# Order of the last expert pages and passes of both MoE layers: down page 30 asked for first, expert 31's gate/up page in halves of k

## What is computed

```python
def expert_block(args):
    xb, e = args
    hb = jax.nn.silu(xb @ w_gate[e]) * (xb @ w_up[e])
    return hb @ w_down[e]
...
    h = h + hierarchical_moe(rmsnorm(h, norm_ffn[layer]), ...)
return rmsnorm(h, final_norm)
```

## Time and profile before

| | |
|---|---|
| median of 3 runs | 1268.96 us (1267.98 to 1270.03) |
| the profiled execution's own time | 1268.41 us |
| its span, first to last instruction | 1266.7 us |
| mean granted TensorE clock | 0.902 of full speed |
| PE busy | 1040.9 us (82%) |
| HBM read | 459.38 MB, 364 GB/s over the span |
| the expert stream of layer 0, its end | about 531 to 569 us |
| the expert stream of layer 1, its end | about 1221 to 1259 us |

### The profile page before, as it was taken

How to read it: one execution, slowest core, us unless ns; L and a number is a source line. 1 busy time by engine, 2 the same in 40 slices (tenths; PEclk the granted TensorE clock), 3 DMA queues, 4 the chain that set the end, 5 groups by cost and what they waited for, 6 DMA issues and landing times.

```text
span 1266.7 us, 22370 instructions
## 1 busy us (share of the span) xinstructions
PE 1040.9 (82%) x9525; PEld 704.6 (56%) x9525; DVE 478.3 (38%) x1230; ACT 234.8 (19%) x526; POOL 4.9 (0%) x27
## 2 busy tenths in 40 slices
PE   9999998866767575889999999999967675758676
PEld 7888755533433342448888888876533333425243
DVE  2342543532223222237665556464343222222223
ACT  2221121111111111103433333121111111111111
POOL 1000000000000000000000000000000000000000
PEclk9999998978788877899999999999988878878789
DMA  9888799999999999996676664899999999999997
GB/s 342 237 338 332 255 419 429 426 428 428 429 429 428 429 429 427 417 394 187 190 231 225 229 223 151 334 361 427 428 427 427 430 428 429 427 429 429 429 419 297
DMA packets 98305, 461.49 MB, mean 364 GB/s; under 512 B 17468, under 2 KB 60728, under 8 KB 73400
## 3 DMA queue, kind: packets, MB, share of 16 engines
q1 hardware_dynamic: 97872, 460.34, 90.5%
q10 hardware_dynamic: 360, 0.15, 0.0%
HBM read 459.38 MB, written 1.08 MB: 364 GB/s over the span
## 4 chain that ended last, share of the span: by engine, by line
PE 51%; DMA 45%; SPq 1%; DVE 1%; issue 1%; ACT 1%; POOL 0%; POOLq 0%; DVEq 0%; ACTq 0%
DMA front<-in_expert_w_up 39%; PE pa L1534 10%; PE pa L1829 8%; PE pb L1534 8%; DMA arena<-in_expert_w_down 5%; PE wa L1829 5%; PE acc L1565 4%; PE wb L1859 3%; PE acc L1684 2%; PE pb L1609 1%; SPq L362 1%; PE pb L1903 1%; PE wa L2124 1%; PE pb L1785 1%; PE acc L1869 1%
## 5 line engine op out<-in xcount | busy, mean ns | idle before, releaser
L1829 PE MATMUL pa<-front,arena 128*32 128x256 f32 x1792 | 126.6, 445 | 80.8 <-DMA front<-in_expert_w_up 80.8
L1289 DVE TENSOR_SCALAR lower<-lower 128x128 f32<-128x128 f32 x64 | 14.4, 225 | 417.6 <-ACT lower L606 417.6
L1829 PE MATMUL wa<-front,arena 128*32 128x256 f32 x1232 | 96.7, 479 | 88.5 <-DMA front<-in_expert_w_up 85.0
L1829 PEld LDWEIGHTS pa<-front,arena 128*32 128x32 f32 x1792 | 63.0, 128 | 146.9 <-DMA front<-in_expert_w_up 93.6
L1829 PEld LDWEIGHTS wa<-front,arena 128*32 128x32 f32 x1232 | 46.1, 136 | 142.1 <-DMA front<-in_expert_w_up 95.0
L606 ACT ACTIVATE arena<-wb 32x256 f32<-32x256 f32 (+2 forms) x236 | 88.9, 377 | 105.0 <-PE wb L1859 96.6
L1859 PE MATMUL wb<-w_dn,conv_raw 128*32 128x256 f32 x1472 | 87.9, 379 | 2.3 <-DMA w_dn<-in_expert_w_down 2.0
L1534 PE MATMUL pa<-hnT,w_x 128*128 128x256 f32 x384 | 85.1, 380 | 0.0
L1829 PE MATMUL wa<-w_x,arena 128*32 128x256 f32 x896 | 64.4, 451 | 19.1 <-DMA w_x<-in_expert_w_up 19.1
L1534 PEld LDWEIGHTS pa<-hnT,w_x 128*128 128x128 f32 x384 | 72.5, 190 | 10.0 <-issue 0.3
L1534 PE MATMUL pb<-hnT,w_x 128*128 128x256 f32 x336 | 74.5, 380 | 0.0
(11 more groups left out here) (345 smaller groups left out, 1252.0 us busy)
## 6 DMA issues: line engine op xcount, KB each, us to landing
w_dn<-in_expert_w_down SPq DMA_DIRECT2D x46, 2048.0 KB, 26.4
front<-in_expert_w_gate SPq DMA_DIRECT2D x42, 2048.0 KB, 19.1
front<-in_expert_w_up SPq DMA_DIRECT2D x42, 2048.0 KB, 23.6
w_x<-in_expert_w_gate SPq DMA_DIRECT2D x15, 2048.0 KB, 32.2
w_x<-in_expert_w_up SPq DMA_DIRECT2D x15, 2048.0 KB, 36.6
arena<-in_expert_w_down SPq DMA_DIRECT2D x14, 2048.0 KB, 25.8
w_x<-in_odd_in_proj SPq DMA_DIRECT2D x16, 1024.0 KB, 5.5
front<-in_expert_w_up SPq DMA_DIRECT2D x10, 1024.0 KB, 8.8
```

Of the source, the lines that this page charges most:

```text
L1289: link(v.tensor_scalar(eg, eg, 1.0, None, ALU.add))
L1829: ins = mm(gu[32 * j:32 * j + 32, :, :], xb[:, k, c0:c0 + CAP], w[k][:, :, P * j:P * j + P], start=(k == 0), stop=(k == KC - 1))
```

## The change

- SP: down 30 is asked for right after up 29, ahead of the wait in `overflow_weights`. After it come gate/up 30, then gate/up 31 in four DMAs of 1024 KB (gate and up for k 0 to 3, then gate and up for k 4 to 7), then down 31 in its two parts.
- PE: gate/up 31 is two passes of half the k, each behind the wait for its half (`gu_res`, `gu_in1`). Down 30 runs ahead of gate/up 31, where the six matmuls on zeros stood, and sum 30 behind gate/up 31.
- ACT: the copy of down 30's result stands ahead of expert 31's exponential.
- SP: the wait for the last part of down 31 before the load of fnorm is gone.

```diff
                 last = [(e, expert_at(l, e)) for e in (NE - 2, NE - 1)]
+                expert_part(l, NE - 2, 2, NE * l + previous(DSLOT, NE - 2), last[0][1])
                 overflow_weights(l)
                 k1 = sp_.value_load(table[0:1, l + 1:l + 2], min_val=0, max_val=OV_LIST)
                 sp_.wait_ge(S["ov_done"], k1 + 1)
-                for parts in ((0, 1), (2,)):
-                    for e, which in last:
-                        for part in parts:
-                            expert_part(l, e, part, NE * l + previous(DSLOT if part == 2 else SLOT, e), which)
+                for part in range(2):
+                    expert_part(l, NE - 2, part, NE * l + previous(SLOT, NE - 2), last[0][1])
+                sp_.wait_ge(S["gu_done"], NE * l + previous(SLOT, NE - 1) + 1)
+                for half in range(2):
+                    k = slice(KC // 2 * half, KC // 2 * half + KC // 2)
+                    for part in range(2):
+                        w = (expert_w_gate, expert_w_up)[part][l, ds(last[1][1], 1), :, :]
+                        sp_.dma_start(w_gu[SLOT[NE - 1]][:, part, k, :],
+                                      w.rearrange("a (p k) f -> p (a k) f", k=KC)[:, k, :]
+                                      ).then_inc(S[("gu_res", "gu_in1")[half]], 16)
+                expert_part(l, NE - 1, 2, NE * l + previous(DSLOT, NE - 1), last[1][1])
...
             sp_.wait_ge(S["gu_done"], 2 * NE - 2)
-            sp_.wait_ge(S["dn_in3b"], 2 * uses(DSLOT, 3, NE) * 16)
             sp_.dma_start(fnorm, final_norm.partition_broadcast(P)).then_inc(S["fnorm_in"], 16)
...
-                    if e == NE - 1:
-                        output_alone(l, e - 1)
+                    if e == NE - 2:
+                        output_alone(l, e)
...
+                    if e == NE - 1:
+                        pe.wait_ge(S["gu_res"], 48 * l + 48)
+                        gate_up(xs, CAP * j, gu_cols(s), GU[e % 2], ks=range(KC // 2))
...
+                    elif e == NE - 1:
+                        gate_up(xs, CAP * j, gu_cols(s), GU[e % 2], ks=range(KC // 2, KC)).then_inc(S["gu_done"], 1)
...
-                    if e and e != NE - 2:
+                    if e and e < NE - 2:
                         down_of(l, e - 1)
...
                     if e == NE - 2:
-                        warm(6)
+                        down_of(l, e)
```

More of the change, by code:

```diff
@@ L1975, in moe @@
                     if e == 3:
-                        pe.wait_ge(S["gu_res"], 16 * l + 16)
+                        pe.wait_ge(S["gu_res"], 48 * l + 16)
                     if e == WIDE:
```

## The result

| | before | changed |
|---|---|---|
| median, same chip | 1269.44 us (12 runs, 1266.91 to 1271.6) | 1273.7 us (12 runs, 1270.12 to 1275.93) |
| ratio | | 1.0031, interval 1.0022 to 1.0041 |
| the profiled execution | 1268.41 us, span 1266.7 | 1273.96 us, span 1272.2 |

The change makes the kernel 2.8 to 5.2 us slower (0.0022 and 0.0041 of 1269.44): 3.9 us by the ratio, 4.3 by the two medians. The forecast was 1271.9, +2.9 us on its own baseline.

The account below looks back on a forecast made before the run. The expert pages' DMA stream was taken to set the pace, with PE waiting. Terms 0.1 + 0.9 - 0.1 + 2.0 = +2.9 us on 1268.96 gave 1271.9 us, range 1269.2 to 1274.4.

Parts of the forecast that it names:

- The stream: Expert pages at layer ends: same bytes and queue, new order, so the last landing stays; 0 us taken.
- the dip: DMA rate falling to 315 and 360 GB/s at SP's return, 0.8 us of missing bytes; filling it counted 0.
- the larger end (0.9 us): Other bound for filling the dip: last landing 0.9 us earlier in layer 0, 0.4 in layer 1.
- Rival 3: Early down 30 fills the dip, later landings come 0.9 and 0.4 us earlier; 1268.6 with clock up, chance 0.10.
- Gate/up 30 lands later: Its page comes third behind up 29; PE idles 2.9 us in layer 0, 1.5 us in layer 1.
- The chain behind it: From gate/up 30 through down 30 and gate/up 31 to down 31's end: +0.1 us layer 0, +0.9 layer 1.
- The clock in layer 0: The 2.9 us gap ahead of gate/up 30 mostly makes that pass slow, by 1.4 to 2.7 us; +2.0 taken.
- Rival 1: The clock stays up in layer 0; total +0.9, 1269.9 us, chance 0.27.
- The clock in layer 1: The 1.5 us gap ahead of gate/up 30 leaves the clock up; 0 taken, 2.7 us as other end.
- Rival 2: The clock falls in both layers; total 4.9, 1273.9 us, chance 0.15.
- The halves "save 1.8 us": Splitting gate/up 31 lets it start before down 30's old landing place; saves 1.8 us on the way.
- The final norm's load: Asked for right behind down 31, it has landed before DVE needs it at the end; -0.1 us, at most -0.2.

Follow-up runs that it names:

- warm_l0: The changed kernel with 12 matmuls on zeros ahead of gate/up 30 in layer 0 only; 1272.71 us, ratio 1.0024 to before.
- whole_page: The changed kernel with gate/up 31 in one piece, without the first half pass and its wait; 1273.80 us, ratio 1.0030 to before.
- down30_early_only: The kernel before with only down 30 asked for ahead of the wait on down pass 27; 1276.06 us, ratio 1.0052 to before.
- fnorm_early_only: The kernel before without the wait on down 31 ahead of the final norm's weight load; 1269.01 us, ratio 0.9995 to before.
- change_third: The changed kernel as it is, profiled a third time; one profile, 1269.59 us.
- halves_only: The kernel before with gate/up 31 as four 1024 KB DMAs and two half passes; 1270.65 us, ratio 1.0011 to before.

## Why the prediction was right, and where it was not

The forecast was slower, +2.9 us; measured +3.9, inside the range, with the mechanism that was named. That the three profiles come to 2.7 is in part luck. In layer 0 they have +0.2 of chain and +1.9 of clock, near the +0.1 and +2.0 of the sum. In layer 1 they have +0.2 of chain, where +0.9 was taken (against before's two ends, one of them 0.8 late), and +0.4 of clock, where 0 was: errors that partly cancel.

- **The stream: right.** The last landing did not move with the dip. The 0 for it holds; the larger end (0.9 us) does not. Over all fourteen profiles, in the seven ends with a dip (some 2 us under 360 GB/s between 8 and 2 us before up 29 lands) it came 29.48 to 30.13 us behind up 29, in 20 of the 21 without one 29.40 to 30.48, in the last 31.09. Rival 3 is out. The Trainium skill ("DMA: Bandwidth & Descriptors", "Rules for kernel authors") advises to issue a DMA early and to wait for it late; here down 30 did come early, and no reader needed it so.
- **Gate/up 30 lands later: right to 0.2 us.** It starts 14.66 to 14.92 us behind up 29, on its page. The gap in layer 0 was foreseen at 2.9 us; it was 2.65 to 4.40, as PE is early there when gate/up 29 runs fast.
- **The chain behind it: right in size.** From gate/up 30's start to the end of down 31 the prediction put 567.6 - 550.9 = 16.7 us for layer 0; in the changed layer 1 it is (1261.53 + 1.07) - 1246.04 = 16.6. The +0.1 of layer 0 was too small by the luck of the baseline: that layer's last landing was the latest of before's four (30.13). Against 29.71 + 2.77 it is 0.5. The +0.9 of layer 1 was too large: up 29 was put at 1226.6 by counting pages back from down 30, but landed at 1226.10, so gate/up 30 came 0.5 us sooner behind it than the sum has. With the clock up it is 32.94 - 32.58 = 0.4.
- **The clock in layer 0: right.** +2.0 was taken, from a slow pass of 1.4 to 2.7; measured 1.3 to 2.5 over 3.66, in three profiles of three. Rival 1 got 0.27 because one row in five had stayed fast; but the five are not alike. The one that stayed fast follows full-size sums, the one at 462.06 matmuls on 32 rows:

```profile
411.81 3.72 PE L1869 MATMUL acc<-arena 128*128 128x256 f32 x16 [0.61 <-ACT arena L606]
418.00 3.66 PE L1829 MATMUL pa<-front,arena 128*32 128x256 f32 x64 [2.48 <-DMA front<-in_expert_w_up]
...
457.98 1.12 PE L1785 MATMUL pb<-arena 32*128 32x512 f32 x2
462.06 6.39 PE L1829 MATMUL wa<-w_x,arena 128*32 128x256 f32 x64 [2.97 <-DMA w_x<-in_expert_w_up]
```

  In the trace of before, of the gate/up passes behind a gap of 1.8 to 2.7 us with the clock up ahead of it, the six that follow matmuls on 32 rows (L1785) are all slow, and four of the six that follow the full-size sums (L1869: 128 rows) are fast; the 2.39 of the earlier trace rows is one of the two that are slow. The gap of the change follows sums on 32 rows; the prediction said so, as an aside and with no row, and did not count its rows by it.
- **The clock in layer 1: the step that was off.** "In layer 1 the gap is 1.5 us ... I take 0." The gap there is 0.87, 1.01 or 2.49 us, as gate/up 29 starts behind its page or on it, and where it is 2.49 the pass is slow. Three more profiles with this page order and no zeros in layer 1 (warm_l0, whole_page, down30_early_only) have 4.38, 1.84 and 3.13 us, and a slow pass each: four of six. Rival 2 (1273.9, chance 0.15) is what happened in the median. The rows for the 0 were too few as well: "the next one up is 2.39" passes over the 2.18 us in the earlier trace rows itself, behind which the pass took 5.35, and the trace of before also holds these two, with the granted clock at 1.00 ahead of both gaps:

```profile
885.01 6.54 PE L1829 MATMUL pa<-w_x,arena 128*32 128x256 f32 x64 [1.46 <-DVE arena L1239]
...
1152.89 5.35 PE L1829 MATMUL wa<-w_x,arena 128*32 128x256 f32 x64 [1.93 <-DMA w_x<-in_expert_w_up]
```

- **The halves "save 1.8 us": not in the change as it runs.** whole_page is as fast. Where the clock stays up they should still save some of it, which no run shows; and alone they open a gap ahead of down 30.
- **The final norm's load: -0.1 was taken, 0 measured.** DVE starts 0.88 us behind the end of sum 31 in both (1259.56 - 1258.68 before, 1265.12 - 1264.24 after); the first square was as late as the load, so taking the load off the path gained nothing.

## What to carry to other kernels

In a stream that is already full, asking for a page earlier only swaps it with the pages behind it: look for the reader of every page that now lands later, and for the gap it leaves on the engine, before counting a gain on the one that lands sooner. A tail that ends on the last landing has its slack set by the last page's time; a pass, its elementwise work and a whole second pass did not fit into it here. And a gap on TensorE is priced at the gap plus the slow pass behind it wherever PE's own chain sets the end, and at nothing where a later landing hides both. A baseline from one profile needs the spread of that gap, not its value in one execution.

## What the runs showed of the hardware that was not expected

- What PE did before a gap tells more of the clock behind it than the gap's length. Counted over all fourteen traces, for gate/up passes behind 1.8 to 2.7 us of idle with the granted clock at 1.00 ahead of it: behind matmuls on 32 rows (the gate rows and the last experts' sums) 74 of 74 ran slow, behind the full-size sums (128*128) 18 of 80, behind zeros 2 of 4. Below 1.4 us of idle none ran slow. No run here changes the work ahead of a gap alone, so this is a count and not an experiment.
- The length alone leaves a wide band: 1.46, 1.84 and 1.93 us were followed by the slow level, 2.48 in the earlier trace rows, 2.67 (gate/up 29 in layer 0 of change_third) and 3.08 us (gate/up 29 in layer 1 of halves_only) were not.
- The rate of 16 engines is a poor witness for when a page has landed: in fnorm_early_only 299 and 360 GB/s in four microseconds, 0.9 us worth of missing bytes at 427, left the last landing where it was (29.65 against 29.70 without the dip).
- The page order of before lands its last page 29.40 to 31.09 us behind up 29 in eight ends, that of the change 29.40 to 30.48 in eighteen: a spread of over 1 us between executions and layers that no edit here explains.
